# Sliding-window value products with two products a block, their halves summed later, and GpSimd in short pieces

## The reference

```python
for l in range(DEPTH):                         # DEPTH = 2
    h = rmsnorm(x, attn_norm_g[l])
    proj = h @ w_in[l]
    qa, ka, va, ga, cq, ckv, kr, gb = jnp.split(proj, SPLIT_POINTS, axis=-1)
    ya = swa_attention(qa, ka, va, swa_sinks[l]) * jax.nn.silu(ga)   # 16 heads of 64, 2 KV heads
    yb = mla_attention(...) * jax.nn.silu(gb)                        # 8 heads of 128
    x = x + jnp.concatenate([ya, yb], axis=-1) @ w_out[l]
...
# swa_attention, per block of 128 queries: keys and values of this block and the one before
probs = jax.nn.softmax(jnp.concatenate([scores, sink], axis=-1), axis=-1)[..., :-1]
out = jnp.einsum('bnhgqk,bnkhd->bnqhgd', probs.astype(v.dtype), vv)
```

## Time and profile before

| | |
|---|---|
| median of 3 runs | 2793.84 us (2792.52 to 2794.48) |
| the profiled execution | 2790.87 us, its span 2789.1 us |
| mean granted TensorE clock | 0.994 of full |
| busy: PE, PEld | 2732.7 us (98%), 2271.2 us (81%) |
| busy: DVE, ACT, POOL | 1241.8 us, 1000.0 us, 1089.6 us |

### The profile page before, as it was taken

One profiled execution on the slowest core, in us unless ns is written; L12 is line 12 of the kernel. 1 busy time (PEld: TensorE's weight loads), 2 busy tenths in 40 slices (PEclk: granted clock), 3 DMA queues, 4 the chain that ended last, 5 costly groups with the idle time before them and its releaser, 6 DMA issues.

```text
span 2789.1 us, 33326 instructions
## 1 busy us (share of the span) xinstructions
PE 2732.7 (98%) x13100; PEld 2271.2 (81%) x13100; DVE 1241.8 (45%) x1831; ACT 1000.0 (36%) x1566; POOL 1089.6 (39%) x544
## 2 busy tenths in 40 slices
PE   8999998999999999899999999999999999999997
PEld 7888887888888888788878888888878888888886
DVE  6466636622346663672335545553443222222223
ACT  5244435523223443553433333332223323332222
POOL 1443332344443433334443333334344444444442
PEclk9999999999999999999999999999999999999998
DMA  6432231254443223124442232222223333336333
GB/s 183 132 84 76 73 121 45 66 142 143 123 132 91 69 76 121 45 67 138 138 120 76 76 83 76 73 80 80 87 83 121 113 109 111 114 113 211 117 125 113
DMA packets 307611, 289.13 MB, mean 104 GB/s; under 512 B 33152, under 2 KB 256000, under 8 KB 306944
## 3 DMA queue, kind: packets, MB, share of 16 engines
q1 hardware_dynamic: 300512, 264.40, 32.0%
q10 hardware_dynamic: 6944, 22.61, 2.1%
HBM read 260.19 MB, written 26.74 MB: 103 GB/s over the span
## 4 chain that ended last, share of the span: by engine, by line
PE 84%; DVE 11%; DMA 2%; ACT 1%; issue 1%; POOL 0%; SPq 0%; DVEq 0%; ACTq 0%
PE bank L873 25%; PE bank L875 24%; PE bank L874 24%; PE work L1131 1%; DMA w_raw<-in_w_in 1%; DVE pt L1728 1%; PE o_bank L874 1%; PE o_bank L875 1%; DVE mixed L1475 1%; PE work L987 1%; PE work L989 1%; PE o_bank L873 1%; DMA latent_scr<-mixed 1%; DVE probs L1680 1%; DVE mixed L1471 1%
## 5 line engine op out<-in xcount | busy, mean ns | idle before, releaser
L850 POOL TENSOR_TENSOR w_lo<-w_raw,w_hi 128x1024 fp32r<-128x1024 f32 (+3 forms) x460 | 982.0, 2137 | 1367.5 <-ACT w_hi L699 1367.5
L873 PE MATMUL bank<-act_in,w_hi 128*128 128x512 f32 x2662 | 1054.0, 396 | 12.8 <-DVE act_in L1443 9.9
L875 PE MATMUL bank<-act_in,w_lo 128*128 128x512 f32 x2662 | 1041.0, 391 | 0.0
L874 PE MATMUL bank<-act_in,w_hi 128*128 128x512 f32 x2662 | 1039.7, 391 | 0.0
L699 ACT ACTIVATE w_hi<-w_raw 128x1024 fp32r<-128x1024 f32 (+3 forms) x468 | 438.0, 937 | 1049.3 <-PE bank L875 648.4
L873 PEld LDWEIGHTS bank<-act_in,w_hi 128*128 128x128 f32 x2662 | 501.0, 188 | 116.8 <-DVE act_in L1443 11.2
L875 PEld LDWEIGHTS bank<-act_in,w_lo 128*128 128x128 f32 x2662 | 500.5, 188 | 107.2
L874 PEld LDWEIGHTS bank<-act_in,w_hi 128*128 128x128 f32 x2662 | 501.2, 188 | 98.9 <-issue 1.7
L873 PE MATMUL bank<-mixed,w_hi 128*128 128x512 f32 x768 | 299.7, 390 | 0.0
L875 PE MATMUL bank<-mixed,w_lo 128*128 128x512 f32 x768 | 299.1, 389 | 0.0
L874 PE MATMUL bank<-mixed,w_hi 128*128 128x512 f32 x768 | 299.0, 389 | 0.0
(11 more groups left out here) (267 smaller groups left out, 2703.7 us busy)
## 6 DMA issues: line engine op xcount, KB each, us to landing
w_raw<-in_w_in SPq DMA_DIRECT2D x512, 128.0 KB, 2.5
w_raw<-in_w_in SPq DMA_DIRECT2D x224, 256.0 KB, 2.9
w_raw<-in_w_out SPq DMA_DIRECT2D x64, 512.0 KB, 3.7
w_raw<-in_w_in SPq DMA_DIRECT2D x32, 512.0 KB, 3.7
w_raw<-in_w_out SPq DMA_DIRECT2D x64, 256.0 KB, 4.6
x_scr<-buf ACTq DMA_DIRECT2D x32, 256.0 KB, 3.2
probs<-x_scr SPq DMA_DIRECT2D x32, 256.0 KB, 5.0
w_raw<-in_w_attn_up SPq DMA_DIRECT2D x32, 256.0 KB, 2.9
```

The costliest lines, as they stand in the source:

```text
L850: nc.gpsimd.tensor_tensor(lo, raw, hi, ALU.subtract).then_inc(lo_ready, 1)
L873: pe.matmul(dst, lhs[0], rhs[0], start=start, stop=False, skip_group_check=skip)
L874: pe.matmul(dst, lhs[0], rhs[1], start=False, stop=False, skip_group_check=skip)
L875: return pe.matmul(dst, lhs[1], rhs[0], start=False, stop=stop, skip_group_check=skip)
```

## The change

Three things are changed. The values of a sliding head lie in `v_swa` as [hi | lo] of 64 columns each, without zeros. A block is multiplied in two matmuls: the 128 columns [hi | lo] by the hi part of the probabilities, which gives hi by hi in rows 0 to 63 of `o_bank` and lo by hi in rows 64 to 127; and the 64 columns hi by the lo part of the probabilities onto rows 0 to 63. Every head starts its own accumulation.

Two new steps follow. "swa_sum", for every head: ACT copies rows 64 to 127 of `o_bank` into `swa_lo` (the tile `sq`), DVE adds it to rows 0 to 63 into the head's half of `swa_sum` (`acc2`) and raises `o_summed`, for which the next head's value product waits. "swa_out", for every pair: DVE multiplies with the gate into `swa_y` (`acc`), ACT copies that into the hi part of the output, POOL subtracts for the lo part and raises `y_done`. They stand 5 and 8 slots behind the transposes, for the last head of a group both stand 3 slots behind.

POOL's lo part of a chunk is issued in pieces of at most 256 columns: four for a usual chunk (and for a "swa" chunk, which had two), at most two for each row tile of the latent groups.

```diff
--- before.py
+++ after.py
@@ -35,6 +35,7 @@
 RAW = 2
 RING = 3
 LO_BY_DVE = 8
+LO_COLS = 256
 MASKED = -1e30
 
 SWA_SCALE = 64.0 ** -0.5
@@ -218,7 +219,8 @@
                 at = (1, 9, 16, 23)[k]
                 turn = at + (6 if k == 0 else 5)
                 head("swa", l, 2 * i + k // 2, k % 2, [(at, "swa_scores"), (at + 2, "swa_norm"), (turn, "transpose"),
-                                                       (turn + 2, "values")])
+                                                       (turn + 2, "values"), (turn + (3 if k == 3 else 5), "swa_sum")]
+                     + ([(turn + (3 if k == 3 else 8), "swa_out")] if k % 2 else []))
         if kind == "mla0":
             head("mla", l, 2 * i, 0, [(1, "mla_scores"), (1, "mla_norm"), (4, "transpose"), (7, "values"),
                                       (10, "output")])
@@ -392,7 +394,8 @@
         y_flat = mixed[:, 8:16, :, :].rearrange("p k s t -> p (k s t)")
         kr_new = y_flat[:, 5 * 2 * T:5 * 2 * T + 3 * T].rearrange("p (n t) -> p n t", n=3)
         k_swa = y_flat[:, 2048:4096].rearrange("p (e s t) -> p e s t", e=2, s=2)
-        v_swa = y_flat[:, 0:1536].rearrange("p (s b c) -> p s b c", s=2, b=NB)
+        v_swa = y_flat[:, 0:1024].rearrange("p (b e s c) -> p b e s c", b=NB, e=2, s=2)
+        swa_lo, swa_sum, swa_y = sq, acc2, acc
         k_sb = y_flat[:, 0:2 * TM].rearrange("p (s t) -> p s t", s=2)
         q_sb = y_flat[:, 1056:2080].rearrange("p (s t) -> p s t", s=2)
         v_sb = y_flat[:, 2080:3104].rearrange("p (s b c) -> p s b c", s=2, b=NB)
@@ -421,6 +424,14 @@
             if kind in ("mix", "gb"):
                 return [(buf[:, 2 * k:2 * k + 2, :], mix_gate(k)) for k in range(2)]
             return [(gate[:, :, :], tmp[:, :, :])]
+
+        def pairs_before(h):
+
+            return 8 * h["l"] + h["h"]
+
+        def swa_heads_before(h):
+
+            return 16 * h["l"] + 2 * h["h"] + h["e"]
 
         def mix_gate(k):
             return (probs, probs2)[k][:, 0:2 * T].rearrange("p (k t) -> p k t", k=2)
@@ -441,6 +452,10 @@
         pt_hi = sem("pt_hi")
         pt_lo = sem("pt_lo")
         pv_done = sem("pv_done")
+        o_lo = sem("o_lo")
+        o_summed = sem("o_summed")
+        swa_gated = sem("swa_gated")
+        swa_hi = sem("swa_hi")
         y_done = sem("y_done")
         y_hi = sem("y_hi")
         v_turned = sem("v_turned")
@@ -817,6 +832,16 @@
                 elif name == "sb_exp":
                     asked()
                     act.activation(probs[:, :], probs[:, :], ACT.Exp).then_inc(probs_ready, 1)
+                elif name == "swa_sum":
+                    h = heads[step[1]]
+                    act.wait_ge(pv_done, h["j"] + 1)
+                    if swa_heads_before(h):
+                        act.wait_ge(o_summed, swa_heads_before(h))
+                    act.activation(swa_lo[0:64, :], o_bank[64:128, :], ACT.Copy).then_inc(o_lo, 1)
+                elif name == "swa_out":
+                    h = heads[step[1]]
+                    act.wait_ge(swa_gated, pairs_before(h) + 1)
+                    act.activation(mixed[:, h["h"], 0, :], swa_y[:, :], ACT.Copy).then_inc(swa_hi, 1)
                 elif name in ("transpose", "transpose2"):
                     h = heads[step[1]]
                     kind = h["kind"]
@@ -835,6 +860,7 @@
         @block.gpsimd
         def _(pool):
             def weight_lo(c):
+
                 pool.wait_ge(hi_ready, c + 1)
                 nk, w = n_k(c), width(c)
                 raw = w_raw[:, c % RAW, 0:nk, 0:w]
@@ -845,9 +871,13 @@
                     raw = raw.rearrange("p k (x a j c) -> p (k x) a j c", x=2, a=2, j=2)
                     hi = hi.rearrange("p k (x j a c) -> p (k x) a j c", x=2, a=2, j=2)
                     lo = lo.rearrange("p k (x j a c) -> p (k x) a j c", x=2, a=2, j=2)
-                    nc.gpsimd.tensor_tensor(lo[:, :, 0], raw[:, :, 0], hi[:, :, 0], ALU.subtract)
-                    raw, hi, lo = raw[:, :, 1], hi[:, :, 1], lo[:, :, 1]
-                nc.gpsimd.tensor_tensor(lo, raw, hi, ALU.subtract).then_inc(lo_ready, 1)
+                    parts = [(slice(None), slice(2 * kx, 2 * kx + 2), a) for a in range(2) for kx in range(2)]
+                else:
+                    parts = [(slice(None), k, slice(at, min(at + LO_COLS, w)))
+                             for k in range(nk) for at in range(0, w, LO_COLS)]
+                for part in parts:
+                    ins = nc.gpsimd.tensor_tensor(lo[part], raw[part], hi[part], ALU.subtract)
+                ins.then_inc(lo_ready, 1)
 
             pool.wait_ge(lo_ready, LO_BY_DVE)
             outputs = 0
@@ -855,6 +885,12 @@
                 name = step[0]
                 if name == "load" and step[1] >= LO_BY_DVE:
                     weight_lo(step[1])
+                elif name == "swa_out":
+                    h = heads[step[1]]
+                    y = mixed[:, h["h"]]
+                    pool.wait_ge(swa_hi, pairs_before(h) + 1)
+                    nc.gpsimd.tensor_tensor(y[:, 1], swa_y[:, :], y[:, 0].bitcast(F32), ALU.subtract
+                                            ).then_inc(y_done, 1)
                 elif name == "output":
                     h = heads[step[1]]
                     y = mixed[:, 8 + h["h"]]
@@ -1142,7 +1178,9 @@
                     h = heads[step[1]]
                     kind, l = h["kind"], h["l"]
                     pe.wait_ge(pt_lo, h["turn0"] + {"swa": 2, "mla": 3, "sb": 4}[kind])
-                    if h["y0"] and h["e"] == 0:
+                    if kind == "swa" and swa_heads_before(h):
+                        pe.wait_ge(o_summed, swa_heads_before(h))
+                    if h["y0"] and (kind != "swa" or h["h"] + h["e"] == 0):
                         pe.wait_ge(y_done, h["y0"])
                     if kind == "swa":
                         pe.wait_ge(v_ready, l + 1)
@@ -1155,14 +1193,19 @@
                         at = PT_AT[kind][j]
                         w = (min(2, NB - j) if kind == "swa" else NB - j) * P
                         if kind == "swa":
-                            v = v_swa[:, :, j, 64 * h["e"]:64 * h["e"] + 128]
+                            both = v_swa[:, j, h["e"], :, :].rearrange("p s c -> p (s c)")
+                            pe.matmul(o_bank[:, j * P:j * P + w], both, pt[:, 0, at:at + w],
+                                      start=j == 0, stop=j == NB - 1, skip_group_check=True)
+                            ins = pe.matmul(o_bank[0:64, j * P:j * P + w], both[:, 0:64], pt[:, 1, at:at + w],
+                                            start=False, stop=j == NB - 1, skip_group_check=True)
+                            continue
                         elif kind == "mla":
                             v = v_mla(h["h"] // 2)[:, :, j, P * (h["h"] % 2):P * (h["h"] % 2) + P]
                         else:
                             v = v_sb[:, :, j, :]
                         ins = three(o_bank[:, j * P:j * P + w], (v[:, 0], v[:, 1]),
                                     (pt[:, 0, at:at + w], pt[:, 1, at:at + w]),
-                                    j == 0 and h["e"] == 0 and kind != "sb", j == NB - 1, skip=True)
+                                    j == 0 and kind != "sb", j == NB - 1, skip=True)
                     ins.then_inc(pv_done, 1)
                 elif name == "pool_mix":
                     c, t = step[1:]
@@ -1628,13 +1671,9 @@
                                         ALU.subtract)
                     vts[0] += 1
                     v.wait_ge(v_turned, vts[0])
-                    link(v.memset(v_swa[:, :, :, 64:128].bitcast(F32), 0.0))
                     src = work[1][:, :].rearrange("p (b a c) -> p b a c", b=NB, a=2)
-                    dst = v_swa.rearrange("p s b (a c) -> p s b a c", a=3)
-                    for e in range(2):
-                        link(v.tensor_copy(dst[:, 0, :, 2 * e, :], src[:, :, e, :]))
-                        link(v.tensor_tensor(dst[:, 1, :, 2 * e, :], src[:, :, e, :],
-                                             dst[:, 0, :, 2 * e, :].bitcast(F32), ALU.subtract))
+                    link(v.tensor_copy(v_swa[:, :, :, 0, :], src))
+                    link(v.tensor_tensor(v_swa[:, :, :, 1, :], src, v_swa[:, :, :, 0, :].bitcast(F32), ALU.subtract))
                     signal(v_ready)
                 elif name == "meta_kv":
                     v.wait_ge(folded, metas[0])
@@ -1731,19 +1770,29 @@
                         v.wait_ge(pt_hi, h["turn0"] + 4)
                         v.tensor_tensor(ptm_sb[64:64 + META, :], o_bank[0:META, :], ptm_sb[0:META, :].bitcast(F32),
                                         ALU.subtract).then_inc(pt_lo, 1)
-                elif name == "output" or (name == "values" and heads[step[1]]["kind"] != "mla"):
+                elif name in ("output", "swa_sum", "swa_out") or (name == "values" and heads[step[1]]["kind"] == "sb"):
                     h = heads[step[1]]
                     kind, t = h["kind"], h["h"]
```

(18 more changed lines are left out.)

## The result

The changed kernel takes 2765.82 us (median of its runs, 2764.67 to 2768.14) beside 2793.84 before: a ratio of 0.9903, interval 0.9889 to 0.9917, so 1.0% or some 27 us faster. Measured a second time, with the experiments, it took 2766.06 beside 2791.25, ratio 0.9910 (0.9896 to 0.9923), 25.2 us. The profiled execution has a span of 2762.8 us, 26.3 less than before.

A forecast was written before the change was run, and what follows sets the result against it. PE, busy 98% of the span, was taken as the bound. Values -15.2, first heads -5.0, latent heads -1.0, late lo parts +1.3, sum and output 0: -19.9 us on 2790.87, median forecast 2774 us, range 2767 to 2784.

The forecast's parts named there:

- The values: Sliding heads' value products on PE: two matmuls a block save 0.475 us a head, 15.2 us in all, bounds 13.5 to 17.
- its 1.6 us: Last narrow block of a sliding head: faster 64-column weight load, estimated at 0.05 us a head, not counted in the forecast.
- The pieces, first heads: PE's waits before transposes of sliding groups' first heads: short POOL pieces shorten DVE's waits, gain 5.0 us, 1.5 to 6.2.
- Latent heads: DVE instruction held up by POOL, PE waiting behind it, in both layers: short pieces gain 1.0 us, 0 to 2.
- POOL late: Lo parts of chunks without margin finish later because pieces take longer and DVE slips in: cost 1.3 us, range 1 to 5.
- The other-side rival: DVE enters between POOL's pieces, so lo parts come late and PE waits: some 2801 us at 3 us late; chance 0.06.
- The sum and output steps: New sum and output work on DVE, ACT and POOL in sliding groups: costed at 0, range 0 to +8 us.
- the chunk's margin of 7 us: At a group's end, the 7.1 us from lo part done to first product was to cover ACT's wait for `swa_gated`.
- the second (2770 us): All first-head waits and part of the latent heads' go, short tiles run a little faster: -24 us; chance 0.12.

## Why the forecast was right in sign and too small in size

**The values: the step that failed.** "The last is followed by a full weight load; I take two thirds of 0.29, 0.19 us." The block took 0.11 to 0.12, and the wide products 0.117 each, not 0.12: 17.5 us in place of 15.2. My own bounds, 7.7 us less and 2.6 more, gave 7.5 to 17.8; I had narrowed them to 13.5 to 17 without a row, and 17.5 lies above. The full-tile kernel shows where it is from: with a 128-column second tile the block takes 0.18 us, about what I had taken, and with the 64-column tile 0.11. The groups of PEld, the weight loads, by form (busy us, mean ns):

```profile
L1197 PEld LDWEIGHTS o_bank<-pt,mixed 128*128 128x128 f32 x128 | 24.0, 188 | 0.3
L1199 PEld LDWEIGHTS o_bank<-pt,mixed 128*64 128x64 f32 x128 | 17.2, 135 | 0.3
```

The narrow tile's load is 53 ns shorter. What that gives shows in the start of the next load, timeline of PEld, first with the full tile, then with the narrow one:

```profile
164.29 0.19 PEld L1199 LDWEIGHTS o_bank<-pt,mixed 128*128 128x128 f32 x1
164.41 0.19 PEld L909 LDWEIGHTS bank<-act_in,w_hi 128*128 128x128 f32 x1
```

```profile
163.31 0.13 PEld L1199 LDWEIGHTS o_bank<-pt,mixed 128*64 128x64 f32 x1
163.37 0.19 PEld L909 LDWEIGHTS bank<-act_in,w_hi 128*128 128x128 f32 x1
```

The load of the next weights starts 0.11 us behind the full tile's and 0.06 behind the narrow one's, and the step from the head's last product to the next is 0.12 us in the one case and 0.05 to 0.06 in the other. The Trainium skill (TensorE: Matmul & The Clock Gate, section LDWEIGHTS) makes the load shorter with the tile's columns, and I had left its 1.6 us out of the sum for want of a row. The difference of the loads, 53 ns, agrees with its 107 and 53 to 1 ns; the durations themselves, 188 and 135 ns, lie about 80 above it.

**The pieces, first heads: right.** -5.0 forecast, -4.4 found there, -4.9 with the smaller steps of the sliding groups. The second group of layer 1 became 0.6 us worse, which comes with the values' change (1.44 us of waiting without pieces, none with pieces alone; its cause I haven't followed), and the others better. With the pieces alone the same eight steps fell by 4.8 us, so the size isn't luck. L1719's longest is 1.54 us (under 1.9) and PE's wait there 0.8 us (under 1.5).

**The pieces, a place that I missed.** The forecast looked for DVE instructions that PE waits for in the attention groups alone. The start of the second block is a third such place, 1.3 us in the profiled executions, and 2.9 to 4.5 when a stretch at half clock follows the wait. The two kernels that differ from the changed one mainly there, pieces in the sliding and gate groups only and pieces of 512, are 4 to 5 us behind it, part of that by the clock.

**Latent heads: given back.** -1.0 forecast; the 1 us in each layer came, and 0.9 of it was lost again one head later. With whole chunks there the time is the same (2766.08 and 2766.06). The step that failed is "gain 1.0 us": it followed the chain to the first wait of PE and not to the next.

**POOL late: a third as much.** +1.3 forecast, +0.4 found (2.7 us of waits for `w_lo`, against the 3.5 to 5 announced). POOL's pieces are 0.81 us on the mean, so its busy time grew by 298 us where 150 to 250 stood: 0.7 us was too little, since DVE enters more often. The other-side rival's mechanism is real, as the kernel with 128 columns shows, but at 256 the entries fall on chunks that have the margin. Counted again, the kernel before has 3 chunks below 0.1 us of margin, 11 below 1.3 and 29 below 3.4 (the forecast said 23); the changed one 4, 8 and 34; the one with 128 columns 13, 20 and 57. What the Trainium skill says of the shared port (SBUF — State Buffer, section Who interferes with whom), that it is held for one instruction, agrees where DVE's normalising and scans go in between two pieces. The forecast's reading of it, that a DVE wait is at most one piece, doesn't hold here: the cast above waited through three ends of 128-column pieces.

**The sum and output steps: right at 0, for a thinner reason.** PE never waits for the sum. But I named the chunk's margin of 7 us as the cover, and the binding thing was another: DVE's evacuation of the bank behind a group's last pair, with less than 1 us to spare. 1.6 us more on DVE there cost 14. Nor is the move of the outputs surely 0: alone it shortened the sliding groups by 2.8 us, step by step, in part at waits that the pieces end as well.

**In all:** 2.3 us from the values and 1.3 from the missed place beyond the forecast, 0.9 less lost to POOL, 0.8 lost at the latent heads, 0.1 less at the first heads: 3.6 of the 6.4 us by which the spans' difference passes the forecast. Of the rest 1.4 is the clock, 0.7 the start, 0.5 the shorter wait for `act_in`, 0.2 small steps. A last term is no work of the kernel at all: I put the median 2.97 us above the profiled execution, as before the change, and it lies 1.15 above it. That is 1.8 of the 8.1 us between forecast and median, more than the 1.2 by which the range was missed; the medians of the kernel before in the later series are 2791.3 to 2791.7, not 2793.84. Of the rivals the second (2770 us) came nearest, and for part of its reason: the short tiles do run faster.

What stays open is how much the clock makes in each execution. In the second series the kernel before took 2788.3 to 2791.3 us at a mean granted clock of 0.995 and 2792.6 to 2794.5 at 0.993. These are the windows of the changed kernel at the first latent head of layer 0:

```profile
418.00:421.00 3.00, 0.20 (x1) 0.20 (x2) 2.66 (x5) 0.38 (x2) 1.77 (x2) 0.99 0.15 38
421.00:424.30 3.30, 3.30 (x11) 2.73 (x11) 0.58 (x1) 2.17 (x4) 0.00 (x0) 0.50 0.16 40
```

PE sits idle for nearly 3 us, then works at 0.50 for 3.4. In this execution there were two such stretches of 3.4 us, in another of the same kernel three, in the kernel before one of 6.8 and one of 3.4; besides, all have one of 22 to 25 us at their end, of which PE works in the first 6 to 8. A stretch of 3.4 us cost up to 1.6 us beside the same steps at 1.00 (at the start of the second block, with 512-column pieces), and differences below about 3 us between two single executions aren't read here as an effect. I made no run that sets the clock apart.

## What to carry to other kernels

Where matmul columns bind, price a removed product by its start-to-start step, and a narrow one by the weight loads around it: a product of 128 columns hid no full load here, so let a narrow product have a narrow tile where it can. Where a helper engine shares a port with one on the path, try cutting its instructions, and not further than the traces bear out; count at every chunk both who waits less and what margin is left, and look at the engine's other instructions too: 1024, 512, 256 and 128 columns gave 2776, 2771, 2766 and 2786 us here. Follow a shortened chain to the next wait but one before its gain is booked, and look at where each block starts, not only at the steps that the change names.

## What the runs showed of the hardware

- 256-column products whose tiles alternate between 128 and 64 columns step at 0.117 us; with full tiles they step at 0.120. Beside a 128-column product the next weight load starts 0.11 us behind a load of 128 columns and 0.06 behind one of 64, and the next product follows suit.
- Undisturbed (the median), a GpSimd subtraction took 0.46 us for 128 columns and 0.74 for 256 in the changed kernel, 1.29 for 512 and 2.40 for 1024 in the one without pieces. Eight short ones beside DVE's scans took 7.33 us, 2.6 times the 2.83 of the single one.
- DVE's two-input instructions went in between two of GpSimd's; a cast of 64x512 did not, through three ends of 128-column ones: 1.77 us, beside 0.43.
- After a PE wait of 1.14 us and 16 products of two columns (2.65 us) the granted clock was 0.50 for 6.8 us in the kernel without pieces; after the same wait in the kernel before it stayed at 1.00. After a wait of 1.9 us ahead of the transposes of a latent head it stayed at 1.00 in one execution of the changed kernel and was 0.50 for 3.4 us in another.
